# Fetching the first weights of two delta-rule regions during the region before and the order of the opening norm

## The reference

```python
def rmsnorm(x, w):
    xf = x.astype(jnp.float32)
    y = xf * lax.rsqrt(jnp.mean(xf * xf, axis=-1, keepdims=True) + EPS)
    return (y * w.astype(jnp.float32)).astype(x.dtype)
...
    for i in range(DEPTH):
        hn = rmsnorm(h, ln_mix[i])
        (g_q, g_k, g_v, g_z, g_a, g_b,
         n_q, n_kc, n_vc, n_ks, n_vs, n_kw, n_vw, n_gate,
         s_q, s_k, s_v) = jnp.split(hn @ w_in[i], SPLIT_POINTS, axis=-1)
        ... (gated delta rule, sparse attention and stick-breaking attention on these pieces)
        h = h + mix @ w_out[i]
        h = h + conv_ffn(rmsnorm(h, ln_ffn[i]), w_up[i], ffn_conv[i], w_down[i])
        gate = jax.nn.sigmoid(rmsnorm(h, ln_ple[i]) @ w_ple_gate[i])
        h = h + gate * rmsnorm(p[i] @ w_ple[i], ple_norm[i])
```

## Time and profile before

| | before |
|---|---|
| median of 3 runs | 3809.13 us (3801.89, 3809.13, 3809.95) |
| the profiled execution's own time | 3803.31 us |
| its span in the trace | 3801.5 us |
| mean granted TensorE clock | 0.948 of full speed |
| PE busy / DVE / ACT / POOL | 3476.1 / 1757.3 / 1307.8 / 417.2 us |
| first opening (layer 0) begins at | 1806.7 us of the span |
| second opening (layer 1) begins at | 2798.6 us of the span |

### The profile page before, as it was taken

How to read it: one execution, slowest core, us unless ns; L and a number is a source line. 1 busy time by engine, 2 the same in 40 slices (tenths; PEclk the granted TensorE clock), 3 DMA queues, 4 the chain that set the end, 5 groups by cost and what they waited for, 6 DMA issues and landing times. The chain is left out here.

```text
span 3801.5 us, 46608 instructions
## 1 busy us (share of the span) xinstructions
PE 3476.1 (91%) x19341; PEld 2725.2 (72%) x19341; DVE 1757.3 (46%) x2690; ACT 1307.8 (34%) x2038; POOL 417.2 (11%) x351
## 2 busy tenths in 40 slices
PE   5989897999999789998988988999989989899998
PEld 4877765788877567887766756788766666677886
DVE  4775465443242534333544354444355434444534
ACT  2332353223232333232422354333343134533423
POOL 0001000120000202200023000221001310012100
PEclk7999998999999899999899899999999989999999
DMA  6651215333221032230310203232122020213231
GB/s 230 199 172 49 78 34 176 125 131 108 81 89 48 9 117 85 83 112 34 109 29 2 63 1 111 78 111 99 69 76 62 2 63 1 89 58 109 79 109 50
DMA packets 230576, 316.70 MB, mean 83 GB/s; under 512 B 13133, under 2 KB 167606, under 8 KB 229086
## 3 DMA queue, kind: packets, MB, share of 16 engines
q1 hardware_dynamic: 230366, 313.72, 25.1%
HBM read 311.04 MB, written 6.85 MB: 84 GB/s over the span
## 5 line engine op out<-in xcount | busy, mean ns | idle before, releaser
L493 PE MATMUL out<-h_lo,w_hi 128*128 128x512 f32 x2608 | 1043.7, 400 | 52.7 <-DVE w_lo L484 48.5
L494 PE MATMUL out<-h_hi,w_hi 128*128 128x512 f32 x2608 | 1022.6, 392 | 0.0
L495 PE MATMUL out<-h_hi,w_lo 128*128 128x512 f32 x2608 | 1021.7, 392 | 0.0
L484 DVE TENSOR_TENSOR w_lo<-ring,w_hi 128x1024 fp32r<-128x1024 f32 (+2 forms) x459 | 561.4, 1228 | 985.5 <-ACT w_hi L479 980.6
L479 ACT ACTIVATE w_hi<-ring 128x1024 fp32r<-128x1024 f32 (+2 forms) x459 | 469.2, 1027 | 1155.1 <-PE out L495 1067.8
L493 PEld LDWEIGHTS out<-h_lo,w_hi 128*128 128x128 f32 x2608 | 493.8, 189 | 177.4 <-issue 60.2
L494 PEld LDWEIGHTS out<-h_hi,w_hi 128*128 128x128 f32 x2608 | 494.1, 189 | 112.6 <-issue 11.0
L495 PEld LDWEIGHTS out<-h_hi,w_lo 128*128 128x128 f32 x2608 | 493.9, 189 | 104.2
L493 PE MATMUL item_banks<-h_lo,w_hi 128*128 128x512 f32 (+1 forms) x632 | 287.8, 455 | 14.3 <-DVE w_lo L484 5.1
L495 PE MATMUL item_banks<-h_hi,w_lo 128*128 128x512 f32 (+1 forms) x632 | 254.6, 403 | 0.0
L494 PE MATMUL item_banks<-h_hi,w_hi 128*128 128x512 f32 (+1 forms) x632 | 254.5, 403 | 0.0
(11 more groups left out here) (503 smaller groups left out, 4649.9 us busy)
## 6 DMA issues: line engine op xcount, KB each, us to landing
ring<-in_mlp_w SPq DMA_DIRECT2D x30, 2048.0 KB, 8.5
ring<-in_w_up SPq DMA_DIRECT2D x44, 1024.0 KB, 7.6
tiles<-in_mod_w SPq DMA_DIRECT2D x80, 512.0 KB, 4.7
ring<-in_e_w_in SPq DMA_DIRECT2D x48, 512.0 KB, 4.2
ring<-in_w_down SPq DMA_DIRECT2D x10, 2048.0 KB, 7.8
ring<-in_w_in SPq DMA_DIRECT2D x16, 1024.0 KB, 5.2
ring<-in_o_w_in SPq DMA_DIRECT2D x7, 2048.0 KB, 7.9
tiles<-in_mod_w SPq DMA_DIRECT2D x8, 1024.0 KB, 8.7
```

The source lines that it names most:

```text
L484: return nc.vector.tensor_tensor(lo.bitcast(F32R), x, hi, ALU.subtract)
L493: nc.tensor.matmul(out, wh, xl, start=start, stop=False, **kw)
L494: nc.tensor.matmul(out, wh, xh, start=False, stop=False, **kw)
L495: return nc.tensor.matmul(out, wl, xh, start=False, stop=stop, **kw)
```

## The change

It has three parts.

1. Load 0 of each opening is no longer fetched into the ring at the region's start. A new lane, `first_load_lane`, issues its four DMAs in the tail before, into 5 of the 32 `tiles`, once those have been read for the last time; PE waits for their arrival at the end of its own program in that tail. The splits of parts 0 to 2 read these tiles and wait for no DMA.
2. In `norm_lane` ACT squares tiles 0, 2, 4, 6 and DVE tiles 1, 3, 5, 7. PE waits for the one or the other semaphore in turn.
3. The planned times: the norm's lane is 2 units long instead of 18, and the three parts stand at 0.5, 0.94 and 0.96. Ln and Exp stand at 0.9.

To make room, `tiles` of the first half is kept for the second one too, and several buffers (`const2`, `by_token`, `sb_v`, `ple`, `y0`) become columns of it. No instruction is added or removed by that.

```diff
@@ norm_lane
-        for f in range(DT):
+        for f in range(0, DT, 2):
             nc.scalar.activation(hT[:, f, :], k.xT[:, f, :], ACT.Square).then_inc(squared, 1)
         yield 0.45
         act.wait_ge(stat_done, 1)
...
         for f in range(DT):
-            pe.wait_ge(squared, f + 1)
+            pe.wait_ge((squared, odd_squared)[f % 2], f // 2 + 1)
             last = nc.tensor.matmul(stat, k.at["ones"], hT[:, f, :], start=(f == 0), stop=(f == DT - 1))
...
     def _(dve):
+        for f in range(1, DT, 2):
+            nc.vector.tensor_tensor(hT[:, f, :], k.xT[:, f, :], k.xT[:, f, :], ALU.mult).then_inc(odd_squared, 1)
         yield 0.55
         dve.wait_ge(rstd_done, 1)
@@ items_lane
     def source(part):
         n, j = parts[part]
-        return ring[:, n % 2, :, j * P:min(j * P + P, widths[n])]
+        load = held if n == 0 and held is not None else ring[:, n % 2, :, :]
+        return load[:, :, j * P:min(j * P + P, widths[n])]
 
     def split_time(part):
         if part < HELD:
+            if firsts_at is not None:
+                return firsts_at[part]
...
         for n, pieces in enumerate(ranges):
+            if n == 0 and held is not None:
+                continue
...
-                act.wait_ge(landed[load % 2], arrived(load))
+                if load or held is None:
+                    act.wait_ge(landed[load % 2], arrived(load))
@@ odd_tail
+        first_load_lane(k, r, r.lane(ch.end - 2.0, 14.0), a, 0, tiles, (mlp_done, 1))
@@ layer_tail, layer 0
+            first_load_lane(k, r, r.lane(gates[1].begin - 20.0, 60.0), a, 1, tiles, (ffn_done, DT))
@@ new
+FIRST_LOAD = [(W_KC + 3 * P, P), (W_KW + P, P), (W_AB, 12), (W_GATE, 18)]
...
+def first_load_lane(k, r, lane, a, l, tiles, hidden_used):
+
+    held, w = first_load_of(tiles), layer_of(a["w_in_2"], l).rearrange("(k p) n -> p k n", p=P)
+    load_in, = r.semaphores("first_load", "load_in")
+
+    @lane.sync
+    def _(sp):
+        yield 0.0
+        sp.wait_ge(*hidden_used)
+        at = 0
+        for col, width in FIRST_LOAD:
+            sp.dma_start(held[:, :, at:at + width], w[:, :, bass.ds(col, width)]).then_inc(load_in, 16)
+            at += width
+
+    @lane.tensor
+    def _(pe):
+        yield 1.0
+        pe.wait_ge(load_in, 16 * len(FIRST_LOAD))
@@ second_mixer
-            norm = r.lane(0.0, BEGIN)
+            norm = r.lane(0.0, 2.0)
...
-            freed, silu_done, _ = items_lane(k, r, r.lane(0.0, 1.0), w, ranges, items, h_ready, ring, w_hi, w_lo, item_banks,
+            freed, silu_done, _ = items_lane(k, r, r.lane(0.0, 1.0), w, ranges, items, h_ready, ring, w_hi, w_lo, item_banks, firsts_at=(0.5, 0.94, 0.96), held=first_load_of(tiles), tap=
```

More of the change, by code:

```diff
@@ L573, in norm_lane @@
     nc = k.nc
-    (squared, stat_done, log_done, rstd_done, scaled, hi_done, h_ready) = r.semaphores(
-        "input", "squared stat_done log_done rstd_done scaled hi_done h_ready")
+    (squared, odd_squared, stat_done, log_done, rstd_done, scaled, hi_done, h_ready) = r.semaphores(
+        "input", "squared odd_squared stat_done log_done rstd_done scaled hi_done h_ready")
     @lane.scalar
     def _(act):
-        for f in range(DT):
+        for f in range(0, DT, 2):
             nc.scalar.activation(hT[:, f, :], k.xT[:, f, :], ACT.Square).then_inc(squared, 1)
@@ L632, in left, with items_lane @@
     return freed[m % 2], m // 2 + 1
-def items_lane(k, r, lane, w, ranges, items, h_ready, ring, w_hi, w_lo, banks, tap=None, bias=None, quick=False, first=0.5):
+def items_lane(k, r, lane, w, ranges, items, h_ready, ring, w_hi, w_lo, banks, tap=None, bias=None, quick=False, first=0.5, firsts_at=None, held=None):
     nc = k.nc
@@ L653, in arrived @@
     def arrived(n):
-        return 16 * sum(len(pieces) for pieces in ranges[n % 2:n + 1:2])
+        return 16 * sum(len(pieces) for pieces in ranges[n % 2 if held is None else n % 2 or 2:n + 1:2])
     def slot(part):
@@ L1278, with __init__ @@
 class Chain:
-    def __init__(self, k, r, blocks, begin, first_part=None):
+    def __init__(self, k, r, blocks, begin, first_part=None, y0=None):
         self.k, self.r, self.blocks, self.first_part = k, r, blocks, first_part
@@ L1284, in __init__ @@
         self.w_hi, self.w_lo = r.sbuf("w_hi", [P, 4 * QUARTER]), r.sbuf("w_lo", [P, 4 * QUARTER])
-        self.rstd, self.y0 = (r.sbuf(name, [P, S])[:, :] for name in ("rstd", "y0"))
+        self.rstd = r.sbuf("rstd", [P, S])[:, :]
+        self.y0 = r.sbuf("y0", [P, S])[:, :] if y0 is None else y0
         self.out = r.psum("out", [P, 8, S])
@@ L3641, in _, with columns_of, first_load_of @@
             nc.scalar.activation(dst, banks[:, j % 2, :], ACT.Copy).then_inc(turn_out, 1)
+def columns_of(tiles, at, count, width):
+    return tiles[:, at:at + count, :].rearrange("p f n -> p (f n)")[:, 0:width]
+FIRST_LOAD = [(W_KC + 3 * P, P), (W_KW + P, P), (W_AB, 12), (W_GATE, 18)]
+def first_load_of(tiles):
+    width = sum(width for _, width in FIRST_LOAD)
+    return columns_of(tiles, 8, 5, DT * width).rearrange("p (k n) -> p k n", k=DT)
+def first_load_lane(k, r, lane, a, l, tiles, hidden_used):
[13 more added lines that the diff above has]
+        pe.wait_ge(load_in, 16 * len(FIRST_LOAD))
 def second_mixer(k, a, l, tiles, gain):
@@ L3652, in second_mixer @@
         ctx.enter_context(split_input(k))
-        const2 = sb("const2_sb", list(a["const2"].shape))
+        const2 = columns_of(tiles, 22, 5, a["const2"].shape[1])
         place(k, const2, second_constants())
         mixing = Region(k)
-        by_token = sb("by_token", [P, TC, 2 * P + 30])
+        by_token = columns_of(tiles, 29, 3, TC * (2 * P + 30)).rearrange("p (c n) -> p c n", c=TC)
         vs_rows, vw_rows, ab = by_token[:, :, 0:P], by_token[:, :, P:2 * P], by_token[:, :, 2 * P:]
-        sq, sk, sv_rows = sb("sb_q", [P, SB_T, S]), sb("sb_k", [P, SB_T, S]), sb("sb_v", [P, TC, N_SB * HD])
+        sq, sk, sv_rows = sb("sb_q", [P, SB_T, S]), sb("sb_k", [P, SB_T, S]), columns_of(tiles, 27, 2, TC * N_SB * HD).rearrange("p (c n) -> p c n", c=TC)
         cols = sb("gdn_cols", [P, 4, TC * N_GDN])
@@ L3664, in second_mixer @@
         k.cos, k.sin = table[:, 0, :], table[:, 1, :]
-        ranges = [[(W_KC + 3 * P, P), (W_KW + P, P), (W_AB, 12), (W_GATE, 18)]]
+        ranges = [FIRST_LOAD]
         ranges += [[(W_GDN + t * 2 * P, 2 * P)] for t in range(2 * GDN_T)]
@@ L3752, in layer_tail @@
         r.stack.enter_context(split_input(k))
-        acc, pn = r.sbuf("temp", [P, DT, S]), r.sbuf("ple", [P, DT, S])
+        acc, pn = r.sbuf("temp", [P, DT, S]), tiles[:, FF_T:FF_T + DT, :]
         p_hi, p_lo = r.sbuf("spare_hi", [P, K, S]), r.sbuf("spare_lo", [P, K, S])
@@ L3774, in layer_tail @@
         gates = [Block("up", up_source(w_gate, [t * COLS]), DT, moving=(k.h_hi, k.h_lo), evac=sigmoid(t), gap=0.0 if t else 8.0) for t in range(2)]
-        ch = Chain(k, r, outs + ups + downs + gates, 12.0, first_part_of(tiles))
+        ch = Chain(k, r, outs + ups + downs + gates, 12.0, first_part_of(tiles), tiles[:, 30, :])
         ch.acc = acc[:, :, :].rearrange("p (u j) n -> p u j n", u=2)
@@ L3956, in place, with first_blocks @@
         at += array.shape[1]
-def first_blocks(k, a):
+def first_blocks(k, a, tiles):
     with ExitStack() as ctx:
@@ L3970, in first_blocks @@
         k.ssd_d = sb("ssd_d", [P, SSD_HEADS])[:, :]
-        tiles = sb("tiles", [P, 32, S])
         even_mixer(k, a, tiles)
@@ L3977, in first_blocks, with second_blocks @@
         odd_tail(k, a, tiles)
-def second_blocks(k, a):
-    with k.sbuf("vec2", [P, V_FCONV + 3 * 2 * FF_T]) as k.vec2, k.sbuf("tiles2", [P, FF_T, S]) as tiles:
+def second_blocks(k, a, tiles):
+    with k.sbuf("vec2", [P, V_FCONV + 3 * 2 * FF_T]) as k.vec2:
         for l in range(2):
@@ L3997, in build @@
         k.xT = sb("xT", [P, DT, S])
+        tiles = sb("tiles", [P, 32, S])
         with split_input(k):
-            first_blocks(k, a)
-        second_blocks(k, a)
+            first_blocks(k, a, tiles)
+        second_blocks(k, a, tiles)
 INS = ["x", "c", "rel_bias", "norm_gains", "mod_w", "mod_b", "mlp_w1", "mlp_w2", "e_w_in", "e_conv_w", "e_conv_b",
```

## The result

| | before | after |
|---|---|---|
| median (20 runs each) | 3808.21 us | 3815.51 us |
| lowest to highest | 3801.89 to 3814.80 | 3807.40 to 3820.72 |
| the profiled execution's own time | 3803.31 us | 3814.12 us |
| its span | 3801.5 us | 3812.3 us |
| mean granted clock | 0.948 | 0.946 |

The ratio is 1.0017, 95% interval 1.0011 to 1.0023: the change costs about 6.5 us (0.0017 x 3808), between 4.2 and 8.8; the medians are 7.3 us apart. It is slower, by less than the 0.2% (7.6 us) that the prediction took as its bound.

A forecast was written before the change was run, and what follows sets the result against it. In the openings, TensorE's sum of squares and the weights' chain were taken to bound the first scaling. Squares and fetch 0, order 2.31 + 1.34 = 3.65 us: 3809.1 + 3.65 = 3812.8 us, range 3803 to 3820.

The forecast's parts named there:

- The bound: Openings: weights and norm chains end nearly together, weights about 1 us later in the second; TensorE, not the squares, bounds the sum.
- Squares on two engines at 0: Sum of squares: DVE's four squares take 2.8 us while it was idle; the sum's end stays, worth 0.
- The fetch at 0: Tails ahead: DMAs land 16 and 45 us before the tails end, so PE's new wait costs nothing.
- Rival 4: Tails: late DMAs hold PE and the barrier, up to 7.6 us more per tail, +18.9 in all; chance 0.04.
- Rival 3: Openings: ACT's DMA waits were the whole matter, 4.16 + 4.06 = 8.2 us faster, 3800.9; chance 0.11.
- Ln and Exp between the parts, +3.65: Openings: first scaling comes 3.96 us behind the sum's end, 2.31 and 1.34 us later, 3.65 us slower in all.
- Items 1 to 3 and all that follows hang on it: Behind item 0: its delay passes on whole to all later work; no later DMA wait absorbs it.
- nothing says that the rise comes later relative to the work: Item 1: clock is low before and after alike, so no extra loss from a later rise was counted.
- rival 1: Item 1: longer pause keeps the clock low another 4 us, 1.8 us per opening, +7.3 in all, 3816.4; chance 0.12.

The follow-up runs named there:

- sq_only: Kernel before with one edit: ACT squares the even tiles, DVE the odd ones; 3811.44 us, ratio 1.0004 to the kernel before.
- fetch_only: Changed kernel with all squares on ACT and all three parts ahead of Ln and Exp; 3805.50 us, ratio 0.9995 to the kernel before.
- the half sum: Changed kernel with only four of the eight sum-of-squares matmuls, so the norm covers half the features; 3808.00 us, ratio 0.9994 to the kernel before.
- order_only: Kernel before with only the new planned times (norm lane 2 units, parts at 0.5, 0.94, 0.96); 3815.47 us, ratio 1.0021 to the kernel before.
- parts_first: Changed kernel with the three parts planned at 0.5, 0.6, 0.7, ahead of Ln and Exp; 3810.09 us, ratio 1.0006 to the kernel before.
- root_first: Changed kernel with all three parts behind Ln and Exp (0.93, 0.94, 0.96); 3821.31 us, ratio 1.0025 to the kernel before.
- pairs: Changed kernel with parts ahead of Ln and Exp, DVE adding squares in pairs, four sum matmuls for eight; 3803.93 us, ratio 0.9986 to the kernel before.
- warm: Changed kernel plus six spare matmuls behind the sum and one behind each of item 0's first seven tiles; 3808.38 us, ratio 1.0000 to the kernel before.
- warm_pause: Changed kernel plus six spare matmuls behind the sum of squares, none in item 0; 3816.84 us, ratio 1.0021 to the kernel before.
- pairs_warm: pairs plus four spare matmuls behind the sum and one behind each of item 0's first seven tiles; 3800.72 us, ratio 0.9974 to the kernel before.
- pairs_pause: pairs plus four spare matmuls behind the sum of squares only; 3805.78 us, ratio 0.9992 to the kernel before.

## Why the prediction was right, and where it was off

- **The bound.** Right. TensorE's sum of squares holds the scaling; the squares don't (sq_only), the DMA only by 0.2 and 1.2 us (fetch_only; about 0.3 and 1 were read from the earlier trace rows), and the half sum brings the scaling in by the time it saves.
- **Squares on two engines at 0.** Right in place: DVE's four take 2.50 us, 0.63 each rather than the 0.69 of the earlier trace rows, and the sum is as long as before. A cost of the total up to 5 us is inside sq_only's interval.
- **The fetch at 0.** Right. SP issues at 1783.22 and 2749.05, some 26 and 53 us ahead of the tails' ends, and PE's wait isn't seen. Rival 4 did not happen. Rival 3, the whole 8.2 us, is refuted by fetch_only: -1.4 us of place, and a total between -5.7 and +1.5. The Trainium skill (DMA: Bandwidth & Descriptors, Rules for kernel authors) says that a DMA's fixed cost overlaps when it is issued early and waited for late. The trace of fetch_only agrees that ACT's wait goes, but its 4.16 us turned into 4.12 us for the sum.
- **Ln and Exp between the parts, +3.65.** Sized nearly right: E to scaling 3.83 and 3.82 us against 3.96 (part 1 to its `w_lo` took 1.07 us, not 1.16, and E to Ln 0.04, not 0.09); the place moved by 2.22 and 1.00 us against 2.31 and 1.34. Part of the second difference is that the sum in that trace ended 0.2 us sooner. That this edit alone makes a loss of this size is shown by order_only; the rest of the change, by parts_first, is worth between -1.1 and +6.1 us. "Items 1 to 3 and all that follows hang on it" holds at T0 + 50 for the two openings together (3.1 us) and for neither alone.
- **The clock.** Here the forecast was short: +3.65 us, measured +6.5, with an interval of 4.2 to 8.8 that just leaves the forecast out. The median, 3815.5 against 3812.8, lies well inside the stated range, but the range owes its width to the scatter of the runs and not to the sum, and a cost of nearly twice the sum falls inside it too. The step that failed is "nothing says that the rise comes later relative to the work", by which rival 1 was left at nothing in the sum. The time at 1.2 GHz grew by 8 us. It did so otherwise than rival 1 said: not 3.6 us in item 1 (items 0 to 3 are 0.94 us shorter in the first opening, 0.90 longer in the second) but, by the difference between runs and trace, for the most part outside the openings, worth about 2.3 us by the balance above. Rival 1's total, 3816.4, is nearer to the result than the forecast's; its mechanism is not. It was also worked out from a misread row: 1829.56 is the end of the window; item 1's first matmul stands at 1830.44.
- **Open.** Whether a later item 0 itself leaves more time at 1.2 GHz far behind it, and why. The runs show more of it in all (order_only and root_first); single traces don't show it apart from what changes between executions. The length of the pause alone doesn't settle the sum: pairs, with 3.70 us of pause, has 412.2 us at 1.2 GHz (standard error 2.6), parts_first and fetch_only with the same pause 404.4 (4.2) and 399.9 (4.6); the trace of pairs has the difference inside the openings (47.1 us in the two times 40, against 36.6).

## What to carry to other kernels

Before fetching early, ask what ends beside the wait: here 8.2 us of waiting for a DMA were worth 1.4 us by place, since the sum of squares ended beside it; shortening that chain as well is what made a faster kernel. In an in-order engine nothing that is ready early may stand behind something that is ready late: two weight splits behind Exp moved the first scaling by 4.6 us, more than the 1.4 us that removing the wait gave. And in a kernel that TensorE bounds, read the time at the low clock beside every result, and where on the path it lies.

## What the runs showed of the hardware

- The granted clock can be at 1.2 GHz in a stretch where another engine sets the pace, and costs nothing there: item 0 of the changed kernel ran at 0.50 and took 9.16 us, at 1.00 in warm it took 9.27.
- Spare matmuls in the pause and in item 0 together kept the clock at 1.00 there, and the total was lower by 8 us (warm against warm_pause, each by its ratio to the kernel before) and by 5 to 7 us (pairs_warm against pairs_pause). In the traces the gain is made in layer 0 between T0 + 100 and T0 + 520: 0.2 us at T0 + 100 and 6.6 at T0 + 520 for warm, 1.1 and 6.8 for pairs_warm. By how much such a gain changes between executions two traces don't tell; the runs' means of the time at 1.2 GHz go the same way (373.9 against 404.4, 369.5 against 402.6).
- The time and the time at the low clock go together: over 233 runs, each taken against the mean of its kernel and session, 0.30 us per us, correlation 0.85.
- The same spare work in an idle pause of TensorE alone held the clock there (1.00 where it had been 0.60) and gained nothing.
